# Seventeen steps of a float32 input projection as three rounded products each, with their operands split on two other engines

## The reference, cut to what matters

```python
h = rmsnorm(x) * (1 + scale1(c)) + shift1(c)          # x: 520 tokens x 1024
z = h @ w_in                                          # 18 chunks of 128 columns, and 24 gate columns
# columns: x-branch 4 chunks, gate branch 4, queries 4, K/V of three attention branches 6
xc = causal_conv(x_branch)                            # width 4
r, i = sigmoid(xc @ wa + ba), sigmoid(xc @ wi + bi)   # block diagonal, 8 blocks of 64
a = exp(-8 * r * softplus(-lam))
u = sqrt(-expm1(2 * log(a))) * i * xc
h_t = a_t * h_(t-1) + u_t                             # RG-LRU, a scan over the prompt's tokens
out = concat(rms(h_t * gelu(gate)), rms(sparse attention of queries, K/V)) @ w_out
x = x + gate1(c) * out                                # then a PEER layer, x += gate2(c) * PEER(...)
```

## Time and profile before

| | |
|---|---|
| median of 3 runs (lowest, highest) | 1778.28 us (1775.96, 1778.42) |
| the profiled execution's own time | 1779.65 us |
| its span, first to last instruction | 1778.0 us |
| mean granted TensorE clock | 0.976 of 2.4 GHz |
| PE busy | 1705.4 us (96%) |
| DVE busy | 1272.3 us (72%) |
| ACT busy | 648.3 us (36%) |
| POOL busy | 377.2 us (21%) |
| HBM read, written | 408.06 MB, 63.37 MB |
| chain that ended last | PE 84%, DVE 8%, DMA 4%, ACT 2% |
| of it, PE at L721 | 7% |

### The profile page before, as it was taken

One profiled execution on the slowest core, in us unless ns is written; L12 is line 12 of the kernel. 1 busy time (PEld: TensorE's weight loads), 2 busy tenths in 40 slices (PEclk: granted clock), 3 DMA queues, 4 the chain that ended last, 5 costly groups with the idle time before them and its releaser, 6 DMA issues.

```text
span 1778.0 us, 30046 instructions
## 1 busy us (share of the span) xinstructions
PE 1705.4 (96%) x11385; PEld 1575.4 (89%) x11385; DVE 1272.3 (72%) x2648; ACT 648.3 (36%) x1023; POOL 377.2 (21%) x375
## 2 busy tenths in 40 slices
PE   7999997789899999999899999999999999999997
PEld 5688776447799999999899999999999999999997
DVE  0213436573387789999899999966888787878786
ACT  1113422672242233333444444443333333333332
POOL 3201020000000001111344444542223222222230
PEclk9999997799999999999999999999999999999998
DMA  9776773300343236766699999999999999999991
GB/s 343 244 233 234 230 233 136 139 1 1 115 164 98 81 104 247 255 222 223 229 354 381 381 382 382 385 381 380 404 388 331 359 331 357 335 351 342 341 325 67
DMA packets 177846, 466.23 MB, mean 262 GB/s; under 512 B 20435, under 2 KB 91603, under 8 KB 176190
## 3 DMA queue, kind: packets, MB, share of 16 engines
q1 hardware_dynamic: 129822, 288.59, 46.0%
q0 software_dynamic: 45168, 173.61, 26.7%
q10 hardware_dynamic: 2736, 2.49, 0.5%
HBM read 408.06 MB, written 63.37 MB: 265 GB/s over the span
## 4 chain that ended last, share of the span: by engine, by line
PE 84%; DVE 8%; DMA 4%; ACT 2%; issue 1%; ACTq 1%; SPq 0%; POOL 0%; DVEq 0%
PE ps L1098 30%; PE ps L984 26%; PE ps L721 7%; PE ps L971 5%; PE ps L924 3%; PE ps L1077 2%; PE ps L623 2%; ACT arena L1141 2%; PE ps L596 1%; PE ps L900 1%; DVE arena L1639 1%; PE ps L892 1%; DVE ul L1774 1%; PE ps L993 1%; DMA gw<-stage 1%
## 5 line engine op out<-in xcount | busy, mean ns | idle before, releaser
L1774 DVE TENSOR_TENSOR ul<-raw,uh 128x1024 fp32r<-128x1024 f32 x256 | 311.9, 1224 | 110.4 <-ACT uh L1141 108.9
L984 PE MATMUL ps<-hh,uh 128*128 128x392 f32 x1024 | 357.4, 349 | 1.6 <-DVE ul L1774 1.6
L984 PE MATMUL ps<-hl,uh 128*128 128x392 f32 x1024 | 349.0, 341 | 0.0
L984 PE MATMUL ps<-hh,ul 128*128 128x392 f32 x1024 | 348.5, 340 | 0.0
L1098 PE MATMUL ps<-ah,ul 128*128 128x392 f32 x1000 | 341.6, 342 | 0.0
L1098 PE MATMUL ps<-al,uh 128*128 128x392 f32 x1000 | 340.8, 341 | 0.0
L1098 PE MATMUL ps<-ah,uh 128*128 128x392 f32 x1000 | 339.5, 339 | 1.0 <-DVE al L1997 1.0
L1141 ACT ACTIVATE uh<-raw 128x1024 fp32r<-128x1024 f32 x256 | 269.9, 1056 | 108.1 <-PE ps L1098 89.7
L528 POOL DMA_INDIRECT xT<-in_u,gidx x128 | 176.4, 1378 | 547.4 <-DVE zg L1822 334.0
L528 POOL DMA_INDIRECT xT<-in_v,gidx x128 | 138.0, 1078 | 377.1 <-DVE vacc L2011 359.4
L984 PEld LDWEIGHTS ps<-hh,uh 128*128 128x128 f32 x1024 | 192.5, 188 | 3.6 <-DVE ul L1774 2.0
(11 more groups left out here) (361 smaller groups left out, 2075.8 us busy)
## 6 DMA issues: line engine op xcount, KB each, us to landing
raw<-in_uT SPq DMA_DIRECT2D x128, 512.0 KB, 5.6
raw<-in_v SPq DMA_DIRECT2D x128, 512.0 KB, 6.6
gw<-stage POOLq DMA_DIRECT2D x28, 896.0 KB, 11.3
gr<-gw SPq DMA_DIRECT2D x32, 784.0 KB, 8.3
zs<-zbuf SPq DMA_DIRECT2D x124, 196.0 KB, 5.8
zin<-zs SPq DMA_DIRECT2D x124, 196.0 KB, 5.8
arena<-in_ada_w SPq DMA_DIRECT2D x32, 512.0 KB, 4.6
arena<-in_w_in SPq DMA_DIRECT2D x18, 512.0 KB, 7.0
```

The lines of the kernel that those rows point to most:

```text
L984: last = mm(ps[:, bank, 0:DN], w[x][:, k * P:(k + 1) * P], m[:, k, G0:TOK], start=(k == 0 and x == 0 and m is hh), stop=(k == KD - 1 and x ...
L1774: tt(ul[:, i % 4, :], raw[:, i % 4, :], uh[:, i % 4, :].bitcast(F32), SUB).then_inc(S["lo_done"], 1)
```

## The change: what it does

1. Steps 1 to 17 of the projection are computed as rounded products: 48 matmuls of float32r a step in place of 16 of float32. Step 0 and the 24 gate columns stay float32. `h` is written to a new place, `hF`. ACT rounds its 8 tiles into `h_hi` (laid over `xT`) and each chunk of weights into `win_hi`; DVE subtracts these from the originals into `h_lo` (laid over the old `hT`) and `win_lo`.
2. The weight chunks have three buffers, and `win_lo` is written in place over the chunk it is taken from. SP loads chunk n+1 where it loaded chunk n. The chunk of step 0 has a place of its own where the table `ohd` lay; `ohd` is loaded again in iteration 17.
3. `gates` goes to `gscratch` in iteration 4 of SP's loop and `gate_rows` comes back in iteration 16, not behind the loop.
4. `kwin` is loaded whole when step 17 is done, and so is POOL's `load_w1`; both lay inside the loop. SP loads 6 of the last 11 pages in iterations 16 and 17, which wait for the recurrence (`lru_dve`), POOL the other 5.
5. On DVE, the turned chunks are added two an iteration at each end, not four together, and at step 2 the difference for step 4 stands ahead of `decay`.

```diff
+            def products(b, weights, moving, ks, ready=None, base=0, every=1):
+                for n, k in enumerate(ks):
+                    if ready is not None and k % every == 0:
+                        pe.wait_ge(ready, base + k // every + 1)
+                    for w, m in ((0, 0), (0, 1), (1, 0)):
+                        for h in range(2):
+                            last = mm(ps[:, b + h, 0:HALF], weights[w](k), moving[m](k)[:, h * HALF:(h + 1) * HALF],
+                                      start=(n == 0 and w == 0 and m == 0), stop=(n == len(ks) - 1 and w == 1))
+                return last
             for n in range(ZC):
-                pe.wait_ge(w_l[n % 2], 16 * (n // 2 + 1))
...
+                else:
+                    pe.wait_ge(S["wql_done"], n)
+                    last = products(2 * (n % 2), [lambda k: win_hi[n % 2][:, k, :], lambda k: win_lo[n % 3][:, k, :]],
+                                    [lambda k: h_hi[:, k, :], lambda k: h_lo[:, k, :]], range(KD),
+                                    ready=S["hl_ready"] if n == 1 else None)
...
+            def high_w(n):
+                act.wait_ge(w_l[n % 3], 16 * (n // 3 + 1))
+                if n >= 3:
+                    act.wait_ge(S["z_ready"], n - 1)
+                fn(win_hi[n % 2], win_w[n % 3], ACT.Copy).then_inc(S["rounded"], 1)
...
+            def low_w(n):
+                dve.wait_ge(S["rounded"], n)
+                tt(win_lo[n % 3], win_w[n % 3], win_hi[n % 2].bitcast(F32), SUB).then_inc(S["wql_done"], 1)
...
-                for i in range(max(4 * (n // 2) - 8, 0), 4 * (n // 2) - 4):
+                for i in range(2 * n - 6 if 4 <= n else 0, 2 * n - 4):
                     shift_m(ADA_HEAD + i)
+                if n <= 4:
+                    low_w(n + 2)
                 if n == 2:
...
                     decay()
...
+                if 6 <= n < ZC - 2:
+                    low_w(n + 2)
                 if 8 <= n <= 14:
                     recur((n - 8) // 2)
+                if n + 3 < ZC:
+                    if n:
+                        for i in (2 * n - 4, 2 * n - 3):
+                            shift_m(ADA_HEAD + i)
+                    low_w(n + 3)
```

More of the change, by code:

```diff
@@ L185, in build @@
         pick = at(46556, 24)
-        win_w = at(13520, 2 * KD, P)
+        win_w = [at(o, KD, P) for o in (38160, 13520, 14544)]
+        win_hi = [wh[:, i, :, :] for i in range(2)]
+        win_lo = [wl0[:, :, :], wl[:, 0, :, :], wl[:, 1, :, :]]
+        hF = at(25872, KD, TOK)
         xpool = at(17680, NB * PAGES, 256)
@@ L356, in _ @@
                 load_tail(2 * n - 3)
+                if n == 4:
+                    sp.wait_ge(S["gates_ready"], 2)
+                    load(io["gscratch"].rearrange("(b h) r -> b (h r)", h=NH), gates[0:NB, 4, :], S["gate_stored"])
+                if n == 16:
+                    sp.wait_ge(S["gate_stored"], 16)
+                    sp.wait_ge(S["att_in"], 1)
+                    for c in range(4):
+                        load(gate_rows[32 * c:32 * c + 16, :], io["gscratch"][16 * c:16 * c + 16], S["gate_moved"])
+                if n >= 16:
+                    sp.wait_ge(S["lru_dve"], 4)
+                    for m in range(3 * n + 5, 3 * n + 8):
+                        page_rows(sp, sel[:, m, :], io["pool_s"], m, S["pages_sync"])
                 if n == 5:
                     load(ohw[0:33], io["ohw"], S["ohw_loaded"])
[L359 to L362, removed]
                 if n == 5:
@@ L367, in _ @@
                              io["wlru"][e], S["lruw_loaded"])
+            sp.wait_ge(S["z_ready"], ZC)
+            load(kwin, io["win_kT"], S["x_loaded"])
             sp.wait_ge(S["ada_ready"], ADA_ALL)
@@ L372, in _ @@
             load(io["o_kv"], zT[:, KC:ZC, :], S["kv_stored"])
[L374 to L381, removed]
             load(vwin, io["win_v"].rearrange("b (c p) f -> p (b c) f", p=P), S["win_loaded"])
             sp.wait_ge(S["lru_dve"], 5)
-            load(io["o_h"], outh, S["lru_stored"])
-            load(io["o_conv"], outc, S["lru_stored"])
+            load(io["o_h"], outh, S["kv_stored"])
+            load(io["o_conv"], outc, S["kv_stored"])
             sp.wait_ge(S["sel_free"], 1)
@@ L962, in _ @@
             pe.wait_ge(S["sk_loaded"], 16)
-            def products(b, weights, moving, ks, first=True, stop=True, ready=None):
-                for n, k in enumerate(ks):
-                    if ready is not None and k % 2 == 0:
-                        pe.wait_ge(ready, k // 2 + 1)
-                    for w, m in ((0, 0), (0, 1), (1, 0)):
-                        for h in range(2):
-                            last = mm(ps[:, b + h, 0:HALF], weights[w](k), moving[m](k)[:, h * HALF:(h + 1) * HALF],
-                                      start=(first and n == 0 and w == 0 and m == 0),
-                                      stop=(stop and n == len(ks) - 1 and w == 1))
-                return last
             def up(b, bank, moved):
@@ L1219, in _ @@
                     copy_m9(ADA_HEAD + 2 * n - 3)
+                if n + 2 < ZC and not 7 <= n <= 13:
+                    high_w(n + 2)
                 if 7 <= n <= 13:
```

94 lines of the change are left out of this document (61 added, 33 removed).

## The result

The change took 1755.16 us in the median of 4 runs (1750.48 to 1758.89), beside 1777.12 (1773.5 to 1778.42, 4 runs) of the kernel before on the same chip: a ratio of 0.9881, 95% interval 0.986 to 0.9901, faster by 1.2% or about 21 us. The range of 1741 to 1764 holds it; the forecast of 1751.4 lies 3.8 us lower. Two of the four runs took 1750.5 and 1751.6 us, the other two 1758.7 and 1758.9. The profiled execution took 1750.48 us, the quickest of the four (span 1748.8, clock 0.978), so its landmarks lie 29 us ahead of those of before, and the medians only 22.

The account below looks back on a forecast made before the run. PE's work was taken to bound the projection loop. Products 22.3 and stalls 6.6, less 2.0 of waits and 1.5 for the tail, plus 1.5 behind the loop, made 26.9 us: 1751.4 us, range 1741 to 1764.

Parts of the forecast that it names:

- The products: Projection steps 1 to 17: rounded matmuls take 5.95 us a step, not 7.26, saving 22.3 us (bounds 20 to 23.5).
- What must be ready: ACT's rounding and DVE's subtracting ahead of each projection step: PE waits cost 2.0 us together (bounds 0.5 and 5).
- The 0.35 us ahead of steps 10 and 12: Projection loop: following ACT's and DVE's queues through gives PE waits of about 0.35 us ahead of these steps.
- the 1.3 us at step 5: Projection loop: DVE, out of `decay`, adds two chunks and subtracts before PE may start, 1.3 us late.
- The two stalls: PE's DMA waits ahead of step 6 and at step 13's tail chunk vanish, saving 6.6 us (bounds 3 and 6.6).
- The tail: Tail chunk loads in the projection loop, still with two slots: 1.5 us allowed for one more stall (bounds 0 and 8).
- Behind the loop: After step 17: gates in time gain 2.3 us, `kwin` lands at about 11 us; 1.5 us gained (bounds -3 and 2.3).
- what would prove me wrong: Signs: products over 6.1 us, waits for `wl` in every step, or `kwin` 3 us late and the clock falling with it.
- The gates: Behind the loop: with `gate_rows` there in time, 2.3 us can be gained of DVE's 4.60 us wait.
- the first: Rival, chance 0.25: PE's clock holds in the attention as idle time ahead shrinks to about 1.1 us; 6 us more, 1745.
- The queues of ACT and DVE: Rival, chance 0.20: they bound the loop; PE waits 1.5 us in each of steps 7 to 14, 12 us, 1763.
- the tail's loads: Rival, chance 0.05: tail chunk landings set the projection step; at 10.7 us landing 57 us lost, about 1808.

Follow-up runs that it names:

- the quarters: The changed kernel with `kwin` loaded in four quarters, the first three issued before step 17 is done: 1756.27 us, beside 1753.05 of the changed kernel.
- the change once more: The changed kernel itself run again with no edit, for the spread of its runs: 1753.2 us, ratio 0.987 to the kernel before.
- B: The changed kernel with the store of `o_kv` and the load of `vwin` waiting for both halves of `load_w1`: 1755.75 us, ratio 0.9881 to the kernel before.
- the added waits: The changed kernel with 23 further PE waits on an existing semaphore ahead of `hidden_prompt`: 1759.86 us in its one run.
- C: The changed kernel with only POOL's bias tables waiting for the window values: 1751.7 us, ratio 0.9876 to the kernel before.
- D: The changed kernel with `kwin`, then all `load_w1` on SP's queue, `o_kv` and `vwin` after those, bias tables after `vwin`: 1750.32 us, ratio 0.9863 to the kernel before.
- A: The changed kernel with POOL's half of `load_w1` waiting until `kwin` has landed: 1761.04 us, ratio 0.9911 to the kernel before.

## Why the prediction was right

**The products** were the term that mattered, and it was 0.9 us too large: 21.4 against 22.3 (bounds 20 to 23.5). The 7.26 us of the earlier trace rows and the 5.95 of the forecast both hold 0.07 us of drain; to the start of the next group the float32 step is 116.92 - 109.73 = 7.19 in the kernel before, as in the run in float32:

```profile
116.92 1.08 PE L596 MATMUL ps<-arena 128*32 128x128 f32 x32
```

So what was off is the rounded step, 5.93 where the row of the `wq` stage has 5.88. How much of the last matmul is counted depends on what stands behind: ahead of gate products, at step 7, the change's step is 132.89 - 127.05 = 5.84 and that of before 146.20 - 139.10 = 7.10, again 1.26 apart. The row was taken from another stage, with another group behind it. The 111 ns a matmul that the prediction takes from the Trainium skill (TensorE: Matmul & The Clock Gate, "Wait — 56ns, not 53.3ns?") would have given 5.3 us a step; 5.93 / 48 is 124 ns, and to go by the row was right.

**What must be ready.** The 0.35 us ahead of steps 10 and 12 came as 0.31 and 0.30, by the forecast's mechanism, seen above: DVE's difference delays the square root, and so ACT's move and sigmoid, for which PE waits. The step that failed is the 1.3 us at step 5. DVE came out of the decay as counted, 7.1 us after step 3 (102.40 to 109.54), but the two additions and the difference behind it ended at 111.07, 8.7 us after step 3, where I had about 10.2: the two additions cost 0.3 us from the end of the decay to the start of the difference (109.54 to 109.85), where the forecast left 1.8 for them. PE began at 111.31 without a gap. The loss was 0.6 us, not 2.0. That such a wait is real when the order is another is what the run with the decay first showed: 7.03 us.

**The two stalls** are gone, 6.6 us forecast; the run in float32 measures 7.3 us between the same landmarks. **The tail** waited 0.70 us at one chunk in the loop, which lengthened that step by 0.9 (127.05 - 118.72 = 8.33 against 7.41), and 0.16 behind step 17, against 1.5 allowed. The loop ended 28.9 us earlier against 25.4. From the end of step 0 to the end of step 17 it is 161.1 - 134.3 = 26.8, and 21.4 + 6.6 - 0.6 - 0.9 = 26.5 are the terms. The other 2.1 are in no term: step 0 ran at the full clock in this execution (7.25 us, and 8.94 before and in the trace beside the quarters) and began 0.4 earlier. That was luck.

**Behind the loop** is where the sum was wrong in substance, and small in size only since errors cancel, which was luck too. I had +1.5 us. From step 17 to L877 it is 282.71 - 215.03 = 67.7 us, before 310.71 - 243.95 = 66.8: -0.9. The pieces, each the change's rows against those of the earlier trace rows and of the same groups before: the window scores begin 12.9 us after step 17 and not 11.1 (-1.7); from them to `hidden_prompt` it is 237.88 - 227.88 = 10.0 and not 6.7, at the lower clock (-3.3); `hidden_prompt` to the next group 10.1 and not 7.9, the late instructions (-2.2); from there to L846 1.2 and not 4.7, since the 3.40 us of PE's wait for ACT are gone (+3.5); and the rest up to L877 2.8 us shorter, since the clock came back within it (L885 4.00 us, before 7.04; the group behind it is slower, 9.53 against 7.50, but a wait of 1.80 for DVE is gone). In the sum -0.9. This differs from execution to execution: the same stretch is 282.83 - 215.85 = 67.0 in the change once more and 281.83 - 216.65 = 65.2 beside the quarters, where the clock did not fall with the wait for the keys: -0.2 and +1.6.
The terms that failed are two. `kwin` landed after 12.7 us where I had 11: 349 GB/s was a rate of the loop, and behind it the DMA engines were full at 201 to 291 GB/s (220 to 230 us). (The quickest 512 KB landed in 3.2 us, not 3.5, which makes the forecast's 11 us 10.7.) And no term held the clock's answer to that wait, which in the profiled execution cost more than the wait; it stood only among what would prove me wrong. The late instructions, 0.16 us before, I did not see.

**The gates.** I counted 2.3 us for them, reasoned from the wait of before. Measured in the order of the changed kernel it is 10.8 us: what a part is worth has to be asked with the other parts in place. Here `kwin` was going to stand ahead of the gates' store.

**The rivals.** The clock fell in the attention, as before, so the first did not come; idle time ahead of that stretch was 2.27 us where it assumed 1.1. The queues of ACT and DVE did not bind, with 0.6 us in the loop; the tail's loads cost 0.9 us, not 57. The profiled execution's 29.2 us (28.0 of them up to L877) exceed the forecast's 26.9; the medians of the change's three sets of runs (22 to 25 us below before) fall short of it by 2 to 5 us. The change's 16 runs lie at 1750.4 to 1755.7, 12 of them, and at 1758.7 to 1761.9, 4. Two profiles of variants at 1755 and 1758 us (B and the added waits) have the clock at 0.50 from 256 to 270 us, where those of the change, of C and of D, with spans of 1747 to 1750, have 0.62; that this parts the two groups is likely and not shown, since none of the upper four has a trace.

## What to carry to other kernels

Ask of a long stretch that one engine fills what each instruction in front of it must wait for, and put the small one (1.2 us here) ahead of the long chain: that order was worth 9 us in the loop and 12 in all, the cheaper arithmetic 21. When a large load moves, look at what small store and load stands behind it on its queue, and price them in the new order. Where an idle time without a releaser stands at the same record in variant after variant, look at the instruction stream and its packets in the DMA view; moving loads did not mend it here.

## What the runs showed of the hardware

- A store of 0.8 KB behind 4.6 MB on the same queue took about 20 us: the issue that waits for it came at 240.33, after 220.61. Before, behind 2.6 MB, it was 9.1 us (246.85 to 255.97).
- 2 MB with 1 MB on the other queue beside it landed after 12.2 to 12.7 us in seven of the rounded kernels' traces, after 13.1 in the float32 run and after 15.0 with the decay first. With that megabyte behind it on its own queue it was 13.7, without it 10.4. A last quarter of 512 KB took as long as the whole. The Trainium skill (DMA: Bandwidth & Descriptors, "Queues, rings and completion order") says that an engine of DMA goes round between the queues packet by packet. For two queues that agrees with A; the same delay on one queue (D) it doesn't explain.
- PE idles up to 3.15 us at a block of 256 instructions, and goes on 1.2 to 1.5 us after a 16 KB packet of instructions has ended. What sets when that packet moves is open. The idle time was 0.16 us before and 1.64 to 3.15 in nine profiles of rounded kernels, also where the transfers were fewer (C); in A it was none.
- A wait for the window keys of 0.68 (the change beside the quarters), 1.09 (C), 1.16 (the added waits) or 1.18 us (the gates behind the loop) was followed by window scores that took 1.92 us, as before the change (1.93). Behind 1.24, 1.28 (B), 1.33, 1.95, 2.70 and 3.52 us they took 2.78 to 3.64. That is one profile each and no rule: in D the clock fell behind 0.62 us at a tail chunk and a further 0.20 us.
